# RWKV-7 inversion on one Trainium2 core: odd chunks on the array's other corners, old values added by identity products

## What is computed

```python
def step(s, inp):
    r_t, w_t, k_t, v_t, a_t, b_t = inp
    sa = jnp.einsum('bhij,bhj->bhi', s, a_t)
    s = s * w_t[:, :, None, :] + sa[..., None] * b_t[:, :, None, :] + v_t[..., None] * k_t[:, :, None, :]
    return s, jnp.einsum('bhij,bhj->bhi', s, r_t)
```

## Time and profile before

| | |
|---|---|
| median of 3 runs | 4082.98 us (4081.25 to 4083.41) |
| the profiled execution | 4082.34 us, span 4080.1 us |
| the RWKV rounds in it | about 2142 to 2685 us of the span |
| first scan copies `r_R` of rounds 2 to 14 | 2249.5 to 2633.4 us: 12 rounds of 32.0 us |
| busy in a round of 32.03 us | PE 30.1, DVE 23.2, ACT 20.6 us |

### The profile page before, as it was taken

One profiled execution on the slowest core, in us unless ns is written; L12 is line 12 of the kernel. 1 busy time (PEld: TensorE's weight loads), 2 busy tenths in 40 slices (PEclk: granted clock), 3 DMA queues, 4 the chain that ended last, 5 costly groups with the idle time before them and its releaser, 6 DMA issues. The chain is left out here.

```text
span 4080.1 us, 84733 instructions
## 1 busy us (share of the span) xinstructions
PE 3834.2 (94%) x35926; PEld 3513.7 (86%) x35926; DVE 2363.4 (58%) x4633; ACT 1554.1 (38%) x2889; POOL 195.1 (5%) x203
## 2 busy tenths in 40 slices
PE   8999999999999999889978999979999999999998
PEld 4889999998888889889976777769876899999997
DVE  4445656432588885348976777646643564444446
ACT  3113222232386653334325666544522531111112
POOL 0000000000011111010000000001111100000000
PEclk9999999999999999999999999989999999999999
DMA  5323223243465544655641111052323121111112
GB/s 210 92 88 91 93 83 96 79 117 120 156 143 167 147 135 137 179 152 179 223 165 34 38 37 42 20 178 86 114 91 118 64 89 46 42 52 42 42 32 86
DMA packets 375542, 418.70 MB, mean 103 GB/s; under 512 B 50474, under 2 KB 317276, under 8 KB 374300
## 3 DMA queue, kind: packets, MB, share of 16 engines
q1 hardware_dynamic: 362927, 368.14, 29.3%
q0 software_dynamic: 7632, 27.84, 2.2%
q10 hardware_dynamic: 4608, 17.30, 1.1%
HBM read 289.10 MB, written 121.77 MB: 101 GB/s over the span
## 5 line engine op out<-in xcount | busy, mean ns | idle before, releaser
L248 PE MATMUL bank<-xn_hi,pw_whi 128*128 128x352 f32 (+1 forms) x2184 | 730.0, 334 | 14.0 <-ACT ring L261 6.2
L248 PE MATMUL bank<-xn_hi,pw_wlo 128*128 128x352 f32 (+1 forms) x2184 | 707.2, 324 | 0.0
L248 PE MATMUL bank<-xn_lo,pw_whi 128*128 128x352 f32 (+1 forms) x2184 | 706.2, 323 | 0.0
L248 PEld LDWEIGHTS bank<-xn_hi,pw_whi 128*128 128x128 f32 (+1 forms) x2184 | 412.8, 189 | 37.2 <-issue 23.1
L248 PEld LDWEIGHTS bank<-xn_lo,pw_whi 128*128 128x128 f32 (+1 forms) x2184 | 414.1, 190 | 3.1 <-issue 1.9
L248 PEld LDWEIGHTS bank<-xn_hi,pw_wlo 128*128 128x128 f32 (+1 forms) x2184 | 412.7, 189 | 1.3
L261 ACT ACTIVATE ring<-bank 128x352 f32<-128x352 f32 (+1 forms) x273 | 126.0, 462 | 439.0 <-PE bank L248 438.4
L3196 PE MATMUL bank<-bx_hi,bp_whi 128*128 128x384 f32 (+1 forms) x768 | 269.8, 351 | 19.0 <-DVE bx_lo L3257 16.8
L1786 PE MATMUL bank<-sum_x_hi,pw_whi 128*128 128x352 f32 x768 | 254.2, 331 | 32.8 <-DVE sum_x_lo L1777 13.9
L233 DVE TENSOR_TENSOR pw_wlo<-ring,pw_whi 128x1024 fp32r<-128x1024 f32 (+1 forms) x92 | 117.6, 1279 | 241.4 <-ACT pw_whi L226 241.0
L3833 PE MATMUL bank<-bx_hi,bp_whi 128*128 128x384 f32 (+1 forms) x768 | 251.2, 327 | 4.7 <-issue 4.7
(11 more groups left out here) (699 smaller groups left out, 10202.2 us busy)
## 6 DMA issues: line engine op xcount, KB each, us to landing
ring<-in_w_in_dram SPq DMA_DIRECT2D x90, 512.0 KB, 4.6
proj_scratch<-ring SPq DMA_DIRECT2D x66, 528.0 KB, 2.9
mm_all<-proj_scratch SPq DMA_DIRECT2D x40, 512.0 KB, 5.9
mm_all<-acum_scratch SPq DMA_DIRECT2D x32, 512.0 KB, 6.6
ring<-in_mlp_w_dram SPq DMA_DIRECT2D x16, 1024.0 KB, 5.5
ring<-in_mlp_w_dram SPq DMA_DIRECT2D x32, 512.0 KB, 3.4
gates_scratch<-ring SPq DMA_DIRECT2D x24, 528.0 KB, 6.6
merged_scratch<-sum_gate ACTq DMA_DIRECT2D x24, 528.0 KB, 4.9
```

Source lines behind the costliest of these rows:

```text
L248: last = self.nc.tensor.matmul(ps[0:n, 0:m], w[:, q, 0:n], self.pair[x][:, q, t0:t0 + m], start=q == 0 and j == 0, stop=q == KD - 1 and j ...
```

## The change

Steps of odd chunks run on the corners of `swapped`, so each step exchanges the halves of their heads; even chunks stay on `heads`. The results of even chunks go to the half's first bank, those of odd chunks to the second, and one instruction reads both banks (`product`). The old value is added by TensorE: an identity product starts the accumulation and the real product is added (`with_itself`), so an engine only copies. Each step is emptied by one engine in one instruction (rows_vd by both). ScalarE's copies after fourth and turn are 128x768 and after square 128x512; VectorE's after eighth and cross1 are 128x512. The last cross product is merged into `cross1` (it also makes F squared), so 10 steps are left. The steps' slots are now written by hand, with none of `Invert` on TensorE in slots 9, 12 and 19.

```diff
--- before.py
+++ after.py
-INVERSION = [("gram", "v"), ("rows_kb", "a"), ("rows_vd", "a"), ("square", "va"), ("fourth", "va"), ("eighth", "va"), ("by8", "v"),
-             ("turn", "va"), ("cross1", "v"), ("cross2", "v"), ("cross3", "v")]
-STEPS = {p + (0 if s == 0 else 2 * s + 1): (s, p) for s in range(len(INVERSION)) for p in range(2)}
-EACH = {w: sum(w in who for _, who in INVERSION) for w in "va"}
+INVERSION = [("gram", "v", 0), ("rows_kb", "a", 3), ("rows_vd", "va", 5), ("square", "a", 7), ("fourth", "a", 10), ("eighth", "v", 13),
+             ("by8", "v", 15), ("turn", "a", 17), ("cross1", "v", 20), ("cross2", "v", 22)]
+STEPS = {at + p: (s, p) for s, (_, _, at) in enumerate(INVERSION) for p in range(2)}
+STEPS_V = {at + p + ("a" in who): (s, p) for s, (_, who, at) in enumerate(INVERSION) if "v" in who for p in range(2)}
+EACH = {w: sum(w in who for _, who, _ in INVERSION) for w in "va"}
...
+        def with_itself(corner, out, weights, y):
+            corner(mm, out, v.eye, y, start=True, stop=False)
+            return corner(mm, out, weights, y, start=False, stop=True)
         for i in range(BATCH):
-            c, q, q2 = p * BATCH + i, slice(i * RC, (i + 1) * RC), slice(2 * i * RC, 2 * (i + 1) * RC)
+            c, at, at2 = p * BATCH + i, slice(i * RC, (i + 1) * RC), slice(2 * i * RC, 2 * (i + 1) * RC)
+            q, odd = i // 2, i % 2
+            e = 2 * odd + q
             AR, B, K, V, A = v.AR[:, z, c, :], v.B[:, z, c, :], v.K[:, z, c, :], v.V[:, z, c, :], v.ABR[:, w, c, 0:RC]
+            out = lambda n: (b1 if odd else b0)[:, n * P + q * RC:n * P + (q + 1) * RC]
+            corner = swapped if odd else heads
             if step == "gram":
-                heads(mm, b0[:, q2], B, AR, start=True, stop=True)
-                last = swapped(mm, b1[:, q2], K, AR, start=True, stop=True)
+                heads(mm, b0[:, at2], B, AR, start=True, stop=True)
+                last = swapped(mm, b1[:, at2], K, AR, start=True, stop=True)
             elif step == "rows_kb":
-                swapped(mm, b0[:, q], K, v.eye, start=True, stop=True)
-                last = heads(mm, b1[:, q], B, v.eye, start=True, stop=True)
+                swapped(mm, b0[:, at], K, v.eye, start=True, stop=True)
+                last = heads(mm, b1[:, at], B, v.eye, start=True, stop=True)
             elif step == "rows_vd":
-                swapped(mm, b0[:, q], V, v.eye, start=True, stop=True)
-                last = heads(mm, b1[:, q], A, v.eye, start=True, stop=True)
+                heads(mm, b0[:, e * RC:(e + 1) * RC], A, v.eye, start=True, stop=True)
+                if odd:
+                    swapped(mm, out(0), A, v.eye, start=True, stop=True)
+                last = swapped(mm, b1[:, P + i * RC:P + (i + 1) * RC], V, v.eye, start=True, stop=True)
             elif step == "square":
-                heads(mm, b0[:, q], A, x.D[:, i, :], start=True, stop=True)
-                last = heads(mm, b1[:, q], x.D[:, i, :], A, start=True, stop=True)
+                corner(mm, out(0), A, x.D[:, e, :], start=True, stop=True)
+                last = corner(mm, out(1), x.D[:, e, :], A, start=True, stop=True)
             elif step == "fourth":
-                heads(mm, b0[:, q2], x.A2[:, i, :], x.DY[:, i, :], start=True, stop=True)
-                last = heads(mm, b1[:, q], x.DY[:, i, 0:RC], x.A2[:, i, :], start=True, stop=True)
+                corner(mm, out(0), x.A[:, e, :], x.D[:, e, :], start=True, stop=True)
+                corner(mm, out(1), x.D[:, e, :], x.A[:, e, :], start=True, stop=True)
+                last = with_itself(corner, out(2), x.A[:, e, :], x.X[:, e, :])
             elif step == "eighth":
-                heads(mm, b0[:, q], x.A4[:, i, :], x.X[:, i, :], start=True, stop=True)
-                last = heads(mm, b1[:, q], x.D4[:, i, :], x.A4[:, i, :], start=True, stop=True)
+                corner(mm, out(0), x.D[:, e, :], x.A[:, e, :], start=True, stop=True)
+                last = with_itself(corner, out(1), x.A[:, e, :], x.X[:, e, :])
             elif step == "by8":
-                last = heads(mm, b0[:, q], x.A8[:, i, :], x.X[:, i, :], start=True, stop=True)
+                last = with_itself(corner, out(0), x.A[:, e, :], x.X[:, e, :])
             elif step == "turn":
-                heads(mm, b0[:, q], x.O[:, i, :], x.X[:, i, :], start=True, stop=True)
-                last = heads(mm, b1[:, q], x.X[:, i, :], v.eye, start=True, stop=True)
+                corner(mm, out(0), x.O[:, i, :], x.X[:, e, :], start=True, stop=True)
+                corner(mm, out(1), x.X[:, e, :], v.eye, start=True, stop=True)
+                last = corner(mm, out(2), x.X[:, e, :], x.O[:, i, :], start=True, stop=True)
+            elif step == "cross1":
+                corner(mm, out(0), x.E[:, e, :], x.F[:, e, :], start=True, stop=True)
+                last = with_itself(corner, out(1), x.F[:, e, :], x.G[:, e, :])
             else:
-                y = x.G[:, i, :] if step == "cross1" else v.N[:, w, c, :]
-                last = heads(mm, (b1 if step == "cross2" else b0)[:, q], x.F[:, i, :], y, start=True, stop=True)
+                last = with_itself(heads, out(0), x.A[:, e, :], x.X[:, e, :])
...
         if slot == 0 and r >= 2:
-        if step == "square":
-            dve.wait_ge(self.as_[p], evacuated(r, s - 1, "a"))
-            tt(x.DY[:, :, RC:2 * RC], x.D[:, :, :], mask(v.eye), ALU.add)
-        dve.wait_ge(self.pes[p], r * len(INVERSION) + s + 1)
+        if "a" in INVERSION[s][1]:
+            dve.wait_ge(self.as_[p], evacuated(r, s, "a"))
+        else:
+            dve.wait_ge(self.pes[p], r * len(INVERSION) + s + 1)
...
-        elif step == "square":
-            last = copy(x.DY[:, :, 0:RC], view(b0))
-        elif step == "fourth":
-            copy(x.D4[:, :, :], wide(b0)[:, :, 0:RC])
-            dve.wait_ge(self.vs[p], evacuated(r, s - 1, "v"))
-            last = tt(x.X[:, :, :], wide(b0)[:, :, RC:2 * RC], x.DY[:, :, RC:2 * RC], ALU.add)
-        elif step in ("eighth", "by8"):
-            dve.wait_ge(self.vs[p], evacuated(r, s - 1, "v"))
-            last = tt(x.X[:, :, :], view(b0), x.X[:, :, :], ALU.add)
-        elif step == "turn":
-            last = copy(x.F[:, :, :], view(b0))
+        elif step == "rows_vd":
+            last = tt(halves(x.X), self.product(p, 0), v.eye2[:, :].unsqueeze(1).broadcast_to([P, 2, P]), ALU.add)
+        elif step in ("eighth", "cross1"):
+            last = copy(x.AX.rearrange("p m (e q) n -> p m e (q n)", e=2), self.product(p, 0, 2).rearrange("p e (m t) -> p m e t", m=2))
+        elif step == "by8":
+            last = copy(halves(x.X), self.product(p, 0))
         else:
-            dve.wait_ge(self.as_[p], evacuated(r, s - 1, "a"))
-            last = tt(N, view(b1 if step == "cross2" else b0), x.G[:, :, :], ALU.add)
+            last = copy(v.N[:, w, c, :].rearrange("p (q e) n -> p e q n", e=2), self.product(p, 0).rearrange("p e (q n) -> p e q n", n=RC))
...
+        copies = lambda t, n, m: activation(t.rearrange("p m (e q) n -> p m e (q n)", e=2),
+                                            self.product(p, n, m).rearrange("p e (m t) -> p m e t", m=m), ACT.Copy)
...
         elif step == "rows_vd":
-            copy(x.D[:, :, :], b1)
-            last = copy(v.V[:, r % 3, c, :], b0)
+            activation(x.D, four(b0[:, 0:BATCH * RC]), ACT.Copy)
+            last = activation(v.V[:, r % 3, c, :], four(b1[:, P:P + BATCH * RC]), ACT.Copy)
         elif step == "square":
-            last = copy(x.A2[:, :, :], b1)
+            last = copies(x.DA, 0, 2)
         elif step == "fourth":
-            last = copy(x.A4[:, :, :], b1)
-        elif step == "eighth":
-            last = copy(x.A8[:, :, :], b1)
+            last = copies(x.DAX, 0, 3)
         else:
-            last = copy(x.G[:, :, :], b1)
+            last = copies(x.FGE, 0, 3)
...
-            x.O, x.D, x.A2, x.A4, x.D4, x.A8, x.X, x.F, x.G = [m[:, i, :, :] for i in range(9)]
-            x.DY = m[:, 9:11, :, :].rearrange("p a b n -> p (a b n)").rearrange("p (i n) -> p i n", n=2 * RC)
+            x.O, x.D, x.A, x.X, x.F, x.G, x.E = [m[:, i, :, :] for i in range(7)]
+            x.DA, x.DAX, x.AX, x.FGE = m[:, 1:3, :, :], m[:, 1:4, :, :], m[:, 2:4, :, :], m[:, 4:7, :, :]
```

More of the change, by code:

```diff
@@ L1046, in vector @@
             nc.vector.tensor_copy(v.eye[h, :], k.ident[h, h])
+            for i in range(2):
+                nc.vector.tensor_copy(v.eye2[h, i * RC:(i + 1) * RC], k.ident[h, h])
             nc.vector.tensor_copy(v.ones[h, :], k.ones64[h, h])
@@ L1113 @@
 HEADS = (slice(0, 64), slice(64, 128))
[L1115 to L1118 removed]
+INVERSION = [("gram", "v", 0), ("rows_kb", "a", 3), ("rows_vd", "va", 5), ("square", "a", 7), ("fourth", "a", 10), ("eighth", "v", 13),
[3 more added lines that the diff above has]
+EACH = {w: sum(w in who for _, who, _ in INVERSION) for w in "va"}
 def evacuated(r, s, who):
[L1123 removed]
+    return r * EACH[who] + sum(who in w for _, w, _ in INVERSION[:s + 1])
```

(37 more changed lines are left out.)

5 lines of the change are left out of this document (1 added, 4 removed).

## The result

| | before | after |
|---|---|---|
| median | 4082.73 us (4081.25 to 4083.41) | 4177.09 us (4173.42 to 4182.76) |
| ratio, 95% interval | | 1.0233 (1.0215 to 1.0251) |
| span of the profiled execution | 4080.1 us | 4175.4 us |
| granted clock, mean | 0.978 | 0.972 |

A forecast was written before the change was run, and what follows sets the result against it. The prediction took TensorE as the bound, with waits for ScalarE also deciding the stage's end. To 4082.3 us it added 23 us of waits (14 x (0.25 + 1.4)) and 17 us of lower clock: 4122 us, range 4082 to 4150.

The forecast's parts named there:

- Slots 0 to 8: Round's stretch up to slot 9: rows_vd's extra units and wider ScalarE copies start slot 9 about 0.25 us later.
- Slot 9: TensorE's idling before slot 9's product, waiting for ScalarE's `r_ST`, grows from 0.78 to about 2.8 us.
- Slot 12: No inversion step covers slot 12 while half 1's fourth is copied: 0.95 to 1.0 us of wait.
- Slots 18 and 19: Waits after turn's wide copy (0.45 us) and for VectorE's `r_R` in the slot empty of inversion (0.4 us).
- The clock: The longer idling drops TensorE to half clock in 12 of 14 rounds, 1.4 us each: +17 us.
- So this stretch changes by its waits alone: Slot 9 to gate product: 76 units on `heads` before and after, so only waits change, +1.4 us per round.
- 0.116 us per unit: Time of one 64x64 float32 product of both heads on one pair of corners; two pairs give two units.
- The two end passes: Passes without the scan or without `Prepare`'s table load: no change, within 1 us each.
- Strict order: Rival: no product starts ahead of an earlier one, 3.5 us more per round, about 4155 us; chance 0.04.
- 4105: Rival: the clock stays up, so only the +23 us of waits counts, 4092 to 4112 us; chance 0.22.
- faster: Rival: slots 12 and 19 find cover and slot 9's gap closes, 4050 us with all 2.3 us gained; chance 0.10.

The follow-up runs named there:

- e1: The kernel after, with two extra unread products on TensorE in slot 9, ahead of the scan's: 4160.28 us, ratio 1.0186.
- e3: The kernel after, with its steps moved up so that slots 9, 12 and 19 are not empty: 4157.01 us, ratio 1.0184.
- e8: e5 with the closed-up slots of e3, output wrong: 4096.85 us, ratio 1.0038 to the kernel before.
- e5: The kernel after, with one wide fixed-table product replacing each odd chunk's two to four narrow ones, square to cross1; output wrong: 4114.78 us, ratio 1.0085.
- e9: The kernel after, with the slots of e3 and part of ScalarE's Prepare (exponentials, logarithm) one slot later: 4157.97 us, ratio 1.019.
- e4: The kernel before, with its steps from fourth on one slot later, leaving slot 9 without an inversion step: 4111.14 us, ratio 1.007.

## Why the prediction was right in direction and wrong in size

- **Slots 0 to 8: right.** +0.25 us per round was forecast, and the stretch grew by 0.21 (12.04 us against 11.83, mean of rounds 2 to 13). In the round shown `r_ST` is copied at 2660.49 behind the wide copy at 2660.02, as the sum had it.
- **Slot 9: right.** 2.70 us of idling at 2660.85, forecast 2.6 to 3.0; it is 2.5 to 2.7 in all 14 full rounds.
- **Slot 12: right.** 1.00 us at 2665.18, forecast 0.7 to 1.0.
- **Slots 18 and 19: partly.** In the round at full clock slot 18's product does not wait, probably because the pause before 2672.48 has already held TensorE while ScalarE went on. The wait of slot 19 for `r_R` is 0.27 us at 2674.09, and was forecast at 0.4 as a pause between passes, which is 0.24 of idling.
- **The clock: right.** 17 us were forecast from twelve falls. There are eleven, they cost 16.9 us by the distance from slot 9 to slot 12, and e1 took 16.8 us away.
- **The step that failed: "So this stretch changes by its waits alone".** From slot 9 on the prediction counted units on the `heads` pair, 76 before and 76 after, and took the swapped pair's products as free. In columns of the array they nearly are. But every product is also an instruction, and these grow from 10644 to 13524 matmul records in twelve rounds, by 27%. The sum took 0.116 us per unit from rows in which two corners stream, and from rows_kb that four corners start together. That is a burst of a few passes; it says nothing of how long four corners can go on. No term bounded it. What the runs showed in its place: 23.7 us of waits for instruction packets in rounds 2 to 13, against 2.5, and 60 us in all between e3 and e8, which have the same slots and the same clock and differ in the number of products. In round 12, at full clock, the round grew by 3.9 us where 1.65 were forecast, and the two pauses, 0.88 and 0.96 us from start to start where 0.06 is normal, are 1.7 of the 2.3 between. That is the mildest round: round 8, at full clock too, takes 36.95 us.
- **The two end passes: wrong for the same reason.** The prediction held the pass without a scan and the pass without `Prepare` at zero, within 1 us each. The first `r_R` comes 4.1 us later than before, and round 14 takes 6.6 us more. In e5 the first is 3.3 us earlier than before and the second 0.2 us longer, so the narrow products cost 7.4 and 6.4 us there.
- **The sum without the narrow products.** In e5 the 14 full rounds are 37 us longer than before's (483.2 against 445.9), and 40 was forecast. With six falls of the clock in place of twelve, worth up to 14 us, some 24 us or more are left for the waits, where the sum had 23. So the terms that were in the sum held. What it lacked is what after has over e5: 62 us (4177 to 4115), of which 48 lie in the full rounds.
- **The rivals.** Strict order did not come true: in the step fourth of half 0, from 2661.13 to 2662.43 in after, `heads` and `swapped` start passes side by side on all four corners, with breaks that cost 0.2 us of the 0.6 that strict order would. That the time of its sum, 4155, lies near after's is no support. The clock does fall, so 4105 is out. Of "faster", the condition was that slots 9 and 12 find cover. e3 gives them cover, takes 20 us off after and is still 1.8% slower than before, which the prediction did not foresee.

In steps from after to before: 62 us for the narrow products (after to e5), of which up to 8.5 us is clock; 18 us for the gaps and their clock (e5 to e8); and 14 us that e8 still has over before.

What stays open is what sets the pace of the packets. Each pause ends at a steady distance behind the end of a packet, so what is missing is the packet. Why the next one follows no sooner than 3.27 us after the last, when it lasts about 1 us, no run shows. The Trainium skill, page "Runtime: NRT & Kernel Launch", under "Instruction fetch mechanics", states that instructions are refilled in 16 KiB blocks of 256 and that the fetching is mostly hidden. The block size agrees with the rows (16 KB, 125 matmuls and about 125 weight loads). That it is hidden holds nearly for before (2.5 us in twelve rounds) and not once four corners run (23.7 us).

## What to carry to other kernels

Where TensorE's work is small products, count its instructions beside its columns, per stretch. A packing that halves the columns' time but adds instructions can be bound by their supply, here at about 37 float32 passes of 64 columns per us with as many weight loads. In this kernel, where the waits ended on "issue", more overlap did not bring the time below 4154 us, and fewer, wider products did. And before a kernel is rebuilt to cut an engine's work, look at the one large wait: here moving four instructions of another engine by a slot gained 0.25%, where the rebuild lost 2.3%.

## What the runs showed of the hardware

- Instructions of TensorE arrive in packets of 16 KB, about 125 matmul records each. In rounds 2 to 13 of the eleven kernels none followed the last in under 3.27 us, though one lasts only about 1 us.
- A wait that the profile puts on "issue" ends 1.2 to 1.7 us after the end of an instruction packet: all 256 of them in rounds 2 to 13 of the eleven kernels.
- Two corners with float32 products of 64 columns need 34.5 records per us and stay under that supply; four need 69 and do not.
- Two pairs of corners overlap, but not without breaks: a step of 8 units on each took the `heads` pair 1.13 us, against 0.93 free and 1.51 in strict order.
- Removing a wait of TensorE can lengthen another that was hidden in it: `r_ST` waits 45.1, 9.1, 4.3 us (after, e3, e9) against issue pauses 23.7, 41.2, 51.5 us.
- An idle stretch of 2.7 us in each round was followed by a granted clock of 0.50 for 3.4 us or more in most rounds (eleven falls); so was one of 2.1 us in the kernel before with one slot moved (e4).
